# First and last turns of two feed-forward networks placed amid the next chunk of matmuls

## The reference, cut to what matters

```
# first block, D_FF = 8192
y = jnp.square(jax.nn.relu(h @ w_ff1)) @ w_ff2
# second block, D_FF_2 = 5632; centred_dwconv3 runs along the tokens, per channel
up = centred_dwconv3(u2 @ ffn_w_up, ffn_conv_w) + ffn_conv_b
a, gv = up[..., :D_FF_2], up[..., D_FF_2:]
h = h + (silu(a) * gv) @ ffn_w_down
```

## Time and profile before

| | us |
|---|---|
| median of 3 runs | 2981.86 (2979.26 to 2983.32) |
| the profiled execution, its own time | 2983.12 |
| its span, first to last instruction | 2981.3 |
| PE busy in it | 2721.1 |
| DVE busy | 1963.0 |
| ACT busy | 1231.2 |
| mean granted clock of PE, share of full speed | 0.965 |

### The profile page before, as it was taken

The page is one execution under the profiler, slowest core; times in us unless marked ns, Lnnn a source line. Parts: engine busy times, 40 slices in busy tenths (PEclk is TensorE's granted clock), DMA queues, the critical chain, the costliest instruction groups (busy, mean ns, idle before and its releaser), DMA issues.

```text
span 2981.3 us, 35099 instructions
## 1 busy us (share of the span) xinstructions
PE 2721.1 (91%) x12877; PEld 2264.0 (76%) x12877; DVE 1963.0 (66%) x2076; ACT 1231.2 (41%) x1281; POOL 74.7 (3%) x36
## 2 busy tenths in 40 slices
PE   0498999898789999999996999999989999999996
PEld 0387978777568888888875788888867888888885
DVE  5768778789656666666666556555555777666666
ACT  1144342444344444444434454444444444444443
POOL 0000000112000000000000000000000000000000
PEclk9599999999889999999998999999999999999998
DMA  8685657666556666666653545766545565666663
GB/s 332 245 245 191 189 147 233 210 205 215 180 193 217 204 218 216 207 211 217 212 161 117 153 141 169 216 199 190 189 144 168 178 195 177 197 189 187 188 189 127
DMA packets 268968, 578.47 MB, mean 194 GB/s; under 512 B 19640, under 2 KB 20560, under 8 KB 263376
## 3 DMA queue, kind: packets, MB, share of 16 engines
q1 hardware_dynamic: 268880, 577.27, 60.9%
HBM read 575.11 MB, written 2.10 MB: 194 GB/s over the span
## 4 chain that ended last, share of the span: by engine, by line
PE 81%; DVE 12%; DMA 2%; ACT 2%; issue 2%; SPq 0%; POOL 0%; DVEq 0%; ACTq 0%; POOLq 0%
PE bank L420 25%; PE bank L421 25%; PE bank L425 24%; PE bank L658 4%; DVE acc L1670 3%; PE bank L655 3%; DVE w_lo L410 2%; DVE acc_w L1602 1%; DVE hg_t L1571 1%; DVE gd_t L1861 1%; DMA early<-in_w_ada 1%; ACT junk L1128 1%; DMA ada_raw<-in_w_ada 1%; DMA raw<-in_w_ff 1%; DVE X L1571 0%
## 5 line engine op out<-in xcount | busy, mean ns | idle before, releaser
L410 DVE TENSOR_TENSOR w_lo<-raw,w_hi 128x1024 fp32r<-128x1024 f32 x880 | 1076.1, 1229 | 723.5 <-ACT w_hi L405 722.3
L405 ACT ACTIVATE w_hi<-raw 128x1024 fp32r<-128x1024 f32 x880 | 930.8, 1059 | 1230.0 <-PE bank L425 1132.0
L420 PE MATMUL bank<-w_hi,op_a_hi 128*128 128x512 f32 x2272 | 904.1, 398 | 8.3 <-DVE op_a_lo L1571 4.4
L421 PE MATMUL bank<-w_hi,op_a_lo 128*128 128x512 f32 x2272 | 891.4, 392 | 0.0
L425 PE MATMUL bank<-w_lo,op_a_hi 128*128 128x512 f32 x2272 | 610.1, 390 | 3.5 <-DVE w_lo L410 3.5
L420 PEld LDWEIGHTS bank<-w_hi,op_a_hi 128*128 128x128 f32 x2272 | 431.7, 190 | 99.3 <-issue 12.6
L425 PEld LDWEIGHTS bank<-w_lo,op_a_hi 128*128 128x128 f32 x2272 | 427.0, 188 | 95.4 <-DVE w_lo L410 6.3
L421 PEld LDWEIGHTS bank<-w_hi,op_a_lo 128*128 128x128 f32 x2272 | 431.4, 190 | 87.6 <-issue 1.0
L420 PE MATMUL bank<-w_hi,hid_hi 128*128 128x512 f32 x864 | 341.4, 395 | 8.9 <-DVE hid_lo L1571 6.4
L421 PE MATMUL bank<-w_hi,hid_lo 128*128 128x512 f32 x864 | 337.6, 391 | 0.0
L425 PE MATMUL bank<-w_lo,hid_hi 128*128 128x512 f32 x864 | 232.1, 391 | 0.0
(11 more groups left out here) (223 smaller groups left out, 1983.9 us busy)
## 6 DMA issues: line engine op xcount, KB each, us to landing
raw<-in_w_in SPq DMA_DIRECT2D x264, 512.0 KB, 4.6
raw<-in_w_ff SPq DMA_DIRECT2D x256, 512.0 KB, 3.8
raw<-in_ffn_w_up SPq DMA_DIRECT2D x176, 512.0 KB, 4.3
ada_raw<-in_w_ada SPq DMA_DIRECT2D x96, 512.0 KB, 5.0
raw<-in_ffn_w_down SPq DMA_DIRECT2D x88, 512.0 KB, 3.8
early<-in_w_ada SPq DMA_DIRECT2D x32, 1024.0 KB, 13.3
raw<-in_w_out SPq DMA_DIRECT2D x32, 512.0 KB, 5.1
ada_raw_f<-in_w_ada SPq DMA_DIRECT2D x32, 512.0 KB, 4.7
```

The lines of the kernel that those rows point to most:

```text
L405: nc.scalar.activation(w_hi[:, gj % RAW], raw[:, j % RAW], ACT.Copy).then_inc(hi_ready, 1)
L410: nc.vector.tensor_tensor(w_lo[:, gj % RAW], raw[:, j % RAW], w_hi[:, gj % RAW].bitcast(F32), ALU.subtract).then_inc(lo_ready, 1)
L420: nc.tensor.matmul(where[:, t], hi(kt + k, tok), w_hi[:, s, k], start=first and k == 0, stop=False)
L421: nc.tensor.matmul(where[:, t], lo(kt + k, tok), w_hi[:, s, k], start=False, stop=False)
```

## The change

Neither the number of matmuls nor that of any other compute instruction changes. One chunk of each network more is written out ahead of PE's loop, which now starts at 2. `up_turning` is a new function: a chunk of 8 pieces with a turn called after the fourth.

- First network: chunk 1 is made in pair 0 instead of pair 2, so that it need not wait for chunk 0 to be taken, and the turn of chunk 0 stands amid it.
- First network, further: the waits on pair 0 and pair 2 count one use more and one less.
- Second network: `turn_up(i, 0)` stands amid the gate part of its own chunk, `turn_up(0, 1)` amid part a of chunk 1, and `turn_up(i, 1)` between passes 0 and 1 of `down2(i-1)` (between 1 and 2 before). The hooks on ACT and DVE follow: the convolution of part a after k = 14 (19 before), that of the gate part after k = 20 (23 before), Silu after k = 20 of the same loop turn (3 of the next), the product after k = 23 (5 of the next).
- The last `down2` reads its operand from buffers of its own, `hid2_end`.

```
-for _name, _n in [("win", (8, 8, 0)), ("out", (4, 4, 0)), ("ffn", (32, 32, 16)),
+for _name, _n in [("win", (8, 8, 0)), ("out", (4, 4, 0)), ("ffn", (33, 32, 15)),
...
+            def up_turning(g, where, turn):
+                for j in range(KP):
+                    piece(pe, g, j, *of(op_a), PK * j, where, j == 0, j == KP - 1)
+                    if j == 3:
+                        turn()
...
             first_chunk(g0, pair(2), 1)
-            turn_hidden(0)
-            with pe.Fori(1, FF1 // CH) as i:
+            pe.wait_ge(taken[0], u_ff[0])
+            up_turning(g0 + 8, pair(0), lambda: turn_hidden(0))
+            down(0, g0 + 8, KP, lambda: turn_hidden(1))
+            with pe.Fori(2, FF1 // CH) as i:
...
             def up2(i, g, turn=None):
...
+                gate_turning(i, g + 8)
+            def gate_turning(i, g):
                 pe.wait_ge(taken[0], before_gate(i))
-                chunk(pe, g, 8, of(op_a), KT, pair(0))
+                up_turning(g, pair(0), lambda: turn_up(i, 0))
...
-            def down2(i, g, gj, last=False, between=None):
+            def down2(i, g, gj, op, last=False, between=None):
                 for c in range(4):
                     x = (c + 1) % 2
-                    if c == 2 and between:
+                    if c == 1 and between:
                         between()
                     if x == 1:
                         pe.wait_ge(taken[1], u_f2[1] + 2 * i + c // 2)
...
-            chunk(pe, g0, 8, of(op_a), KT, pair(0))
-            turn_up(0, 0)
-            turn_up(0, 1)
-            with pe.Fori(1, FF2 // CH) as i:
+            gate_turning(0, g0 + 8)
+            up2(1, g0 + 16, lambda: turn_up(0, 1))
+            down2(0, g0 + 16, 16, hid2, between=lambda: turn_up(1, 1))
+            with pe.Fori(2, FF2 // CH) as i:
...
 # ACT, second network
-                hooks = {3: lambda: silu_up(i - 1), 7: lambda: round_hidden2(i - 1, g),
-                         11: lambda: take_up(i, 0, g + 8), 19: lambda: take_up(i, 1, g + 16)}
+                hooks = {3: lambda: round_hidden2(i - 1, g), 11: lambda: take_up(i, 0, g + 8),
+                         19: lambda: take_up(i, 1, g + 16), 20: lambda: silu_up(i)}
...
 # DVE, second network
-                hooks = {5: lambda: product_up(i - 1), 9: lambda: low_hidden2(i - 1),
-                         19: lambda: conv_up(i, 0, cva, f2["cva"]),
-                         21: lambda: add_down(X, i, 0, g + 18),
-                         23: lambda: (add_down(X, i, 1, g + 20), conv_up(i, 1, cvg, f2["cvg"]))}
+                hooks = {5: lambda: low_hidden2(i - 1), 14: lambda: conv_up(i, 0, cva, f2["cva"]),
+                         20: lambda: conv_up(i, 1, cvg, f2["cvg"]), 21: lambda: add_down(X, i, 0, g + 18),
+                         23: lambda: (product_up(i), add_down(X, i, 1, g + 20))}
```

More of the change, by code:

```diff
@@ L1068, in _, with up2 @@
             u_f2 = USES["ffn2"]
-            def up2(i, g):
+            def up2(i, g, turn=None):
                 pe.wait_ge(taken[2], u_f2[2] + i)
-                chunk(pe, g, 0, of(op_a), KT, pair(2))
+                if turn:
+                    up_turning(g, pair(2), turn)
+                else:
+                    chunk(pe, g, 0, of(op_a), KT, pair(2))
+                gate_turning(i, g + 8)
+            def gate_turning(i, g):
                 pe.wait_ge(taken[0], before_gate(i))
-                chunk(pe, g, 8, of(op_a), KT, pair(0))
+                up_turning(g, pair(0), lambda: turn_up(i, 0))
             def before_gate(i):
                 return u_f2[0] if isinstance(i, int) and i == 0 else u_f2[0] + 3 * i - 2
-            def down2(i, g, gj, last=False, between=None):
+            def down2(i, g, gj, op, last=False, between=None):
                 pe.wait_ge(f2["hi"], i + 1)
@@ L1091, in down2 @@
                         pe.wait_ge(taken[0], u_f2[0] + 3 * i + (1 if last else 2) + c // 2)
-                    chunk(pe, g, gj + 2 * c, of(hid2), 4, pair(x))
+                    chunk(pe, g, gj + 2 * c, of(op), 4, pair(x))
             def turn_up(i, k):
@@ L1108, in _ @@
             first_chunk(g0, pair(2), 3)
[L1109 to L1113 removed]
+            gate_turning(0, g0 + 8)
+            up2(1, g0 + 16, lambda: turn_up(0, 1))
+            down2(0, g0 + 16, 16, hid2, between=lambda: turn_up(1, 1))
+            with pe.Fori(2, FF2 // CH) as i:
                 up2(i, g0 - 8 + 24 * i)
[L1115 to L1117 removed]
+                down2(i - 1, g0 - 8 + 24 * i, 16, hid2, between=lambda: turn_up(i, 1))
+            down2(FF2 // CH - 1, g0 + 256, 0, hid2_end, last=True)
         @block.scalar
@@ L1392, in relu_up @@
             def relu_up(i, g):
+                first = isinstance(i, int)
+                x, n = (0, 1) if first and i == 1 else (2, i + 1 if first else i)
                 act.wait_ge(w_used, g + KP)
                 act.wait_ge(ff["made"], i)
-                f(relu[:], pair(2), ACT.Relu, taken[2])
-                act.wait_ge(taken[2], USES["ffn"][2] + i + 1)
+                f(relu[:], pair(x), ACT.Relu, taken[x])
+                act.wait_ge(taken[x], USES["ffn"][x] + n)
                 f(relu[:], relu[:], ACT.Square, ff["act"])
@@ L1529, in silu_up, with round_hidden2 @@
                 f(sga[:], cva[:], ACT.Silu, f2["e"])
-            def round_hidden2(i, g):
+            def round_hidden2(i, g, op=hid2):
                 act.wait_ge(f2["h"], i + 1)
-                act.wait_ge(w_used, g)
-                f(hid2[0][:], sga[:], ACT.Copy, f2["hi"])
+                if g is not None:
+                    act.wait_ge(w_used, g)
+                f(op[0][:], sga[:], ACT.Copy, f2["hi"])
             hi_pieces(s0, g0, 16, {11: lambda: take_up(0, 0, g0 + 8)}, RAW)
@@ L1549, in _ @@
             n = FF2 // CH - 1
-            hi_pieces(s0 + 256, g0 + 256, 8, {1: lambda: silu_up(n), 3: lambda: round_hidden2(n, g0 + 256)})
+            hi_pieces(s0 + 256, g0 + 256, 8, {1: lambda: round_hidden2(n, None, hid2_end)})
             exp_ln_tables()
```

22 lines of the change are left out of this document (13 added, 9 removed).

## The result

The changed kernel takes **2995.58 us** (median of 6 runs, 2988.51 to 2998.64) beside 2983.51 for the kernel before (6 runs, 2979.26 to 2987.13): a ratio of 1.004, 95% interval 1.003 to 1.005. It is slower, by 12 us.

What follows compares the result with a forecast made beforehand. TensorE, busy 91% of the span, was taken as the bound. Terms -24.2 + 1.7 + 25 + 2.7 + 15 = +20.2 on 2983.1 gave 3003.3, so 3002 us for the median; range 2984 to 3008.

Steps and rivals of the forecast that it cites:

- Ten waits behind the second convolution, +25: Second network: TensorE's pass 2 waits 2.5 us for VectorE's `add_down` of pass 0, in each of 10 turns.
- The clock, +15: Behind 8 in 10 of the 11 new TensorE waits, a stretch at 1.2 GHz costing 1.7 us each.
- The first rival: The waits come but the clock stays: +5.2 or, with no exit cost, +2.5, 2984 to 2987 us; chance 0.12.
- What is removed, -24.2: Three TensorE waits in the two feed-forward networks go: 18.56 us of waiting and 5.62 of slow matmuls.
- the second network's share of the forecast: Removed at its start: 5.57 us waiting, 2.00 slow matmuls; at its end: 6.58 waiting, 1.48 slow matmuls.
- First network, +1.7: Chunk 1's first piece is rounded late, so TensorE starts at 860.23 instead of 858.58.
- the landing: First network: chunk 1's first piece lands by DMA at an unmoved time, since SP's list is not changed.
- Exit of the loop, +2.7: Second network: TensorE's idle time on leaving its loop, until then hidden in the 6.41 us wait, shows as 2.67.
- The bound of 0: Second network's loop exit: lower bound of its cost, nothing of it need come; the upper bound was 2.67.

Runs made afterwards that it cites:

- the first experiment: Changed kernel with VectorE's add of pass 0 ahead of the second network's second convolution and that of pass 1 ahead of a low half and the product: 2948.71 us.
- the unrolled build: Kernel before with one more chunk of each network written out ahead of PE's loop, same order, nothing moved: 2976.10 us, ratio 0.9977.
- the second profile: Both kernels run once more, unchanged, one run each: the kernel before 2982.99 us, the changed kernel 2989.06 us.
- fourth: Kernel of the first experiment with the second network's last block in `hid2` again, without its own buffer: 2956.88 us, ratio 0.9908.
- the second experiment: Changed kernel with VectorE's add of pass 0 right behind the second convolution, ahead of the low half that stood between: 2973.28 us, ratio 0.9967.

## Why the prediction was right, and where its sum was not

The forecast was 3002 and slower; 2995.58 came, inside the range, from the mechanism named. Step by step:

- **Ten waits behind the second convolution, +25.** Right in place, number and size. The chain took 9.00, not 8.85, since the convolution starts 1.24 and not 1.08 behind the turn. A loop turn grew from 67.10 to 70.01 where the clock stayed: 2.9 for a wait forecast at 2.5. Ten such waits, the first one shorter by 0.46 (2.15 and 2.61), come to some 28.6. Moving the add ahead took them all away. (The turn of 67.10 is the distance of two starts of `turn_up(i, 1)` in the kernel before, 2789.28 and 2856.38, and in the first experiment, 2825.31 and 2892.41.)
- **The clock, +15.** Nine of ten waits and the one in the first network have a slow stretch, at 1.60: 16 instead of 15. The first rival, that the clock stays, fell with it. By the Trainium skill, page "TensorE: Matmul & The Clock Gate", section "HAM oscillation — how this bites in real kernels", which warns only of longer gaps, these waits should have cost nothing but themselves; the trace does not agree, 0.72 behind nine waits of 2.15 to 2.62.
- **What is removed, -24.2.** Right: the stretch with the second network, without the ten waits, is 740.3 in the first experiment (its exit wait of 1.03 included) and 755.9 in the unrolled build, 15.6 less, and the second network's share of the forecast was 5.57 + 2.00 + 6.58 + 1.48 = 15.6. Against the kernel before itself (754.7) it is 14.4: the slow stretch behind the last wait is 1.5 longer in the unrolled build (23.85 from that matmul to the last group, 22.33 before). So the exact 15.6 is met in part by chance.
- **First network, +1.7.** 2.29 came. The forecast held that the landing would not move; the first piece was rounded 859.17 - 834.92 = 24.25 behind the network's first matmul before and 852.41 - 827.65 = 24.76 after, 0.5 later. In the second profile of the changed kernel the wait is 1.57 instead of 2.12, and has no slow stretch behind it.
- **Exit of the loop, +2.7.** This step failed: 0 came. It read the 2.50 us of "issue" in the earlier trace rows as something a loop's end costs. It was a wait for `hid_lo`, which the first network's tail makes late. In the second network `hid2_end` has its low half ready in time (2954.75, with TensorE there at 2956.47). The bound of 0 was named, the reason for it was not. Where the ten waits don't hold TensorE back, 1.03 of wait comes at this place with the buffer (first experiment) and 2.51 without it (fourth).
- **What no step had: the start.** A build with the chunks written out and nothing moved is faster by 7 us. The forecast argued from the code around the change and took the rest of the program for untouched, though the change writes out a chunk more of each network.

With the measured sizes the sum is -24.2 + 2.3 + 28.6 + 0 + 16 = 22.7. The two windows gave 20.4 against the kernel before, and give 21.3 against the unrolled build (1367.8 + 781.9 - 1372.5 - 755.9); by the medians the changed kernel stands 2995.58 - 2976.10 = 19.5 above it, where +20.2 was forecast. The traces close the gap between the 22.7 and the windows. Against the kernel before: its 2.50 us wait at the first network's exit has a slow stretch behind it, the same wait in the changed kernel has none, and from that matmul to the transposes of `XN` the two take 51.62 (1537.17 to 1588.79) and 49.99 (1525.31 to 1575.30). That is 1.6 by chance of the clock, and 0.6 more differs between there and the second network: 22.7 - 2.2 = 20.5. Against the unrolled build the longer slow stretch at its end gives 22.7 - 1.5 = 21.2. Against the kernel before, the start pays back 7.1 of the 19.5, and 12 is left. So the median missed by 6 us for a cause outside the forecast's steps; inside them, waits and clock were too small by 4 to 5 and the exit too large by 2.7. That 19.5 and 20.2 agree so closely is partly luck: these errors, and the chance of the clock, cancel in part.

## What to carry to other kernels

When a step moves ahead of another on an in-order engine, write down for whom each step behind it is due, and put the one that TensorE waits for first: here the same change gains 34 us or loses 12, by the place of two adds (27 and 19.5 against a build of the same shape with nothing moved). Count a wait of TensorE twice, by itself and by the clock behind it: of the loop's waits, those of 2.6 us mostly paid both prices here, those of 1.5 only the first. And compare a change with a build that has its shape but not its moves, when the effect is within some tenths of a per cent.

## What the runs showed that was not expected

- Waits of 1.04 to 1.51 us in the second network had no slow stretch behind them in ten cases of ten (granted clock 1.00 over 2290 to 2945 of the second experiment); waits of 2.15 to 2.62 had one in nine of ten in the changed kernel, in both its profiles, and waits of 2.18 to 2.64 in ten of ten with the second network's edits alone.
- The length of a wait does not settle it. The wait of 2.49 to 2.50 us at the first network's exit stands in eleven of the thirteen profiles; six have a slow stretch behind it (0.72), five have none. In the changed kernel, the wait and the 6 us from its end:

```profile
1525.31 0.47 PE L421 MATMUL bank<-w_hi,hid_hi 128*128 128x512 f32 x1 [2.49 <-issue]
```

```profile
1525.31:1531.31 6.00, 6.00 (x26) 4.96 (x27) 2.26 (x2) 1.24 (x2) 0.00 (x0) 1.00 0.31 100
```

  From that matmul to the transposes of `XN`, the six take 51.6 and the five 50.0: again 1.6 for a slow stretch. What decides between the two, here and at the wait that ends at 2802.33, is open.
- A wait costs more than its row shows: 2.61 shown, 2.9 in the length of the loop turn; 1.50 shown, 2.0 (69.14 - 67.10). Of this, 0.17 is in the drawing: the four matmuls ahead of it show as 1.07 and take 0.90.
- A label of "issue" hid a wait for a low half made by VectorE twice (2.50 and 1.03 us); the row of the producer, ending 0.10 us ahead of TensorE, told it.
- Writing out more of a loop that runs in the last two thirds of the program moved the end of VectorE's first wait for `w_ada` from 31.46 us (34.30 in the second profile) to 26.23, and shortened the whole by 7 us.
